# Swapping the head halves of the rotary step by DMA instead of by a permutation matmul

## What is computed

```python
def apply_rope(x, cos, sin):              # x: (..., 64) per head and map
    x1, x2 = x[..., :32], x[..., 32:]
    return concatenate([x1 * c - x2 * s, x1 * s + x2 * c], axis=-1)

qa = apply_rope(qa.reshape(S, 8, 64), cos, sin)
ka = apply_rope(ka.reshape(S, 8, 64), cos, sin)
s = einsum('bqhmd,bkhmd->bhmqk', qa, ka) * scale     # scores of differential attention
```

## Time and profile before

| what | value |
|---|---|
| median of 3 runs | 1937.48 us (1933.66 to 1937.8) |
| the profiled execution's own time | 1934.02 us |
| its span | 1932.2 us |
| TensorE busy | 1889.2 us (98%) |
| VectorE busy | 1299.9 us (67%) |
| ScalarE busy | 921.7 us (48%) |
| GpSimd busy | 233.2 us (12%) |
| mean granted TensorE clock | 0.993 |
| DMA | 177.20 MB, mean 92 GB/s |

### The profile page before, as it was taken

One profiled execution on the slowest core, in us unless ns is written; L12 is line 12 of the kernel. 1 busy time (PEld: TensorE's weight loads), 2 busy tenths in 40 slices (PEclk: granted clock), 3 DMA queues, 4 the chain that ended last, 5 costly groups with the idle time before them and its releaser, 6 DMA issues.

```text
span 1932.2 us, 31506 instructions
## 1 busy us (share of the span) xinstructions
PE 1889.2 (98%) x11358; PEld 1647.4 (85%) x11358; DVE 1299.9 (67%) x1910; ACT 921.7 (48%) x1589; POOL 233.2 (12%) x207
## 2 busy tenths in 40 slices
PE   7999999999999999999999999999999999999998
PEld 6899988778878889998888999888776788999886
DVE  6789832667555678983267989435796677999423
ACT  4355522427556445552243555333387543555323
POOL 2100000220224210000021000002156221000001
PEclk8999999999999999999999999999999999999999
DMA  4132332312211213233222232322321022333321
GB/s 156 66 116 102 112 128 87 102 68 71 94 44 45 87 67 120 98 115 124 87 88 88 88 114 103 131 87 88 115 72 45 21 70 85 110 109 109 119 99 44
DMA packets 36574, 177.20 MB, mean 92 GB/s; under 512 B 12544, under 2 KB 14080, under 8 KB 16016
## 3 DMA queue, kind: packets, MB, share of 16 engines
q1 hardware_dynamic: 35040, 173.76, 26.3%
q10 hardware_dynamic: 1264, 1.80, 0.3%
q0 software_dynamic: 192, 0.59, 0.1%
HBM read 174.04 MB, written 2.10 MB: 91 GB/s over the span
## 4 chain that ended last, share of the span: by engine, by line
PE 92%; DVE 3%; ACT 2%; POOL 1%; issue 1%; DMA 1%; SPq 0%; ACTq 0%; POOLq 0%; DVEq 0%
PE ps L352 29%; PE ps L354 28%; PE ps L353 28%; PE ps L1622 1%; DVE wl L286 1%; ACT wh L282 1%; PE ps L1645 1%; PE ps L1152 1%; PE ps L1224 1%; POOL xg L2461 1%; POOL acc L439 1%; DMA raw<-in_units 1%; PE ps L1351 0%; PE ps L1214 0%; PE ps L1134 0%
## 5 line engine op out<-in xcount | busy, mean ns | idle before, releaser
L352 PE MATMUL ps<-xgh,wh 128*128 128x256 f32 (+1 forms) x1504 | 513.8, 342 | 12.7 <-DVE wl L286 5.1
L354 PE MATMUL ps<-xgh,wl 128*128 128x256 f32 (+1 forms) x1504 | 506.8, 337 | 0.0
L353 PE MATMUL ps<-xgl,wh 128*128 128x256 f32 (+1 forms) x1504 | 506.2, 337 | 0.0
L286 DVE TENSOR_TENSOR wl<-raw,wh 128x2048 fp32r<-128x2048 f32 (+1 forms) x92 | 212.7, 2312 | 359.1 <-ACT wh L282 359.1
L352 PE MATMUL ps<-tmh,wh 128*128 128x256 f32 (+1 forms) x1344 | 411.5, 306 | 0.0
L353 PE MATMUL ps<-tml,wh 128*128 128x256 f32 (+1 forms) x1344 | 410.6, 305 | 0.0
L354 PE MATMUL ps<-tmh,wl 128*128 128x256 f32 (+1 forms) x1344 | 410.1, 305 | 0.0
L282 ACT ACTIVATE wh<-raw 128x2048 fp32r<-128x2048 f32 (+1 forms) x92 | 174.5, 1898 | 364.7 <-PE ps L354 363.2
L352 PEld LDWEIGHTS ps<-xgh,wh 128*128 128x128 f32 x1504 | 286.2, 190 | 48.0 <-DVE wl L286 6.1
L353 PEld LDWEIGHTS ps<-xgl,wh 128*128 128x128 f32 x1504 | 286.1, 190 | 30.1 <-issue 2.2
L354 PEld LDWEIGHTS ps<-xgh,wl 128*128 128x128 f32 x1504 | 286.2, 190 | 29.8
(11 more groups left out here) (310 smaller groups left out, 2584.3 us busy)
## 6 DMA issues: line engine op xcount, KB each, us to landing
raw<-in_units SPq DMA_DIRECT2D x160, 1024.0 KB, 4.9
out<-xg SPq DMA_DIRECT2D x4, 512.0 KB, 4.0
relb<-in_rpb SPq DMA_DIRECT2D x64, 24.0 KB, 2.1
x<-in_xT ACTq DMA_DIRECT2D x2, 512.0 KB, 5.9
raw<-in_units SPq DMA_DIRECT2D x4, 256.0 KB, 6.5
x<-in_xT SPq DMA_DIRECT2D x2, 512.0 KB, 8.0
cosA<-in_rope_a ACTq DMA_DIRECT2D x1, 256.0 KB, 2.6
sinA<-in_rope_a ACTq DMA_DIRECT2D x1, 256.0 KB, 2.9
```

Of the source, the lines that this page charges most:

```text
L286: nc.vector.tensor_tensor(wl[:, c % 2, 0:n], raw[:, c % 2, 0:n], wh[:, c % 2, 0:n].bitcast(F32), ALU.subtract).then_inc(w_lo, 1)
L352: nc.tensor.matmul(dst, lh, rh, start=first, stop=False, skip_group_check=onto)
L353: nc.tensor.matmul(dst, lh, rl, start=False, stop=False, skip_group_check=onto)
L354: return nc.tensor.matmul(dst, ll, rh, start=False, stop=last, skip_group_check=onto)
```

## The change

The permutation products on TensorE are left out. Instead, ScalarE issues four DMAs for each block, each from 32 partitions of `q32` to the 32 partitions that hold the other half of the head, into a new buffer `rq` with two slots. The minus sign moves into the sine table, on the host. VectorE's multiplication by the sine table reads `rq` from SBUF where it read PSUM. The load of `permA` is left out, so the semaphore of the tables counts to 48.

```diff
-        permA = sb("permA", [P, P], F32, diff_mem)
+        rq = sb("rq", [P, 2, SEQ], F32, diff_mem)
...
-        rot_done = sem("rot_done")
+        rot_in = [sem("rot_in0"), sem("rot_in1")]
...
-        def rot_pe(pe, i):
-            pe.wait_ge(q32_done, i + 1)
+        def rot_act(act, i):
+            act.wait_ge(q32_done, i + 1)
             if i >= 2:
-                pe.wait_ge(qs_done, i - 1)
-            nc.tensor.matmul(ps[:, 2 + i % 2, :], permA[:, :], q32[:, i % 2, :],
-                             start=True, stop=True).then_inc(rot_done, 1)
+                act.wait_ge(qs_done, i - 1)
+            for r in range(0, P, 32):
+                o = r ^ 32
+                act.dma_start(rq[r:r + 32, i % 2, :], q32[o:o + 32, i % 2, :]).then_inc(rot_in[i % 2], 16)
...
-            for dst, src in ((cosA, rope_a[0:P, :]), (sinA, rope_a[P:2 * P, :]), (permA, perm_d[:, 0:P])):
+            for dst, src in ((cosA, rope_a[0:P, :]), (sinA, rope_a[P:2 * P, :])):
...
-                rot_pe(pe, i - 2)
-            rot_pe(pe, 6)
...
-                    if v == 0 and t == 0:
-                        rot_pe(pe, 7)
...
                 if i == 1:
                     act.wait_ge(lam_done, 2)
                     nc.scalar.activation(col(C_LAM, 2), col(C_LAM, 2), ACT.Exp).then_inc(lam_exp, 1)
+                rot_act(act, i)
                 if i >= 1:
                     qa_hi_act(act, i - 1)
...
-            dve.wait_ge(rot_done, i + 1)
+            dve.wait_ge(rot_in[i % 2], 64 * (i // 2 + 1))
...
-            nc.vector.tensor_tensor(qs[:, i % 2, :], ps[:, 2 + i % 2, :], sinA[:, :], ALU.mult).then_inc(qs_done, 1)
+            nc.vector.tensor_tensor(qs[:, i % 2, :], rq[:, i % 2, :], sinA[:, :], ALU.mult).then_inc(qs_done, 1)
...
+    turn_sign = np.ones((2 * P, 1), np.float32)
+    turn_sign[P:][np.arange(P) % 64 < 32] = -1.0
...
-        "ident": np.eye(P, dtype=np.float32), "perm": perm, "rope_a": rope_rows(64, P, 0),
+        "ident": np.eye(P, dtype=np.float32), "perm": perm, "rope_a": rope_rows(64, P, 0) * turn_sign,
```

More of the change, by code:

```diff
@@ L1797, in even_pe @@
             norm_pe(pe, 1, 4)
-            pe.wait_ge(even_in, 64)
+            pe.wait_ge(even_in, 48)
             for i in range(2, 8):
@@ L1847, in even_act @@
                     norm_act(act, 1, 4)
-                    act.wait_ge(even_in, 64)
+                    act.wait_ge(even_in, 48)
                 if i == 1:
@@ L1921, in even_dve @@
         def even_dve(dve):
-            dve.wait_ge(even_in, 64)
+            dve.wait_ge(even_in, 48)
             nc.vector.tensor_tensor(lamp, lamb.rearrange("p (a b e) -> p a b e", a=2, b=2)[:, :, 0, :],
@@ L2051, in even_pool @@
         def even_pool(pool):
-            pool.wait_ge(even_in, 64)
+            pool.wait_ge(even_in, 48)
             for i in range(8):
```

## The result

| | kernel before | changed kernel |
|---|---|---|
| median of 9 runs each | 1937.44 us | 1940.96 us |
| lowest and highest | 1932.92 to 1938.04 | 1939.12 to 1941.72 |
| ratio, with 95% interval | | 1.0026 (1.0017 to 1.0035) |
| profiled execution: time, span | 1934.02, 1932.2 | 1940.2, 1938.4 |

The change makes the kernel slower by 0.26% of its time, which is some 5 us, by the ratio, and by 3.5 us by the medians. My forecast was 1938.5 us with a range of 1933.5 to 1943.0.

The account below looks back on a forecast made before the run. The prediction took TensorE as the bound, with VectorE arriving together at the first scores. VectorE's chain 1.1 us later plus 1.7 for a clock fall made +2.8 us on 1935.7: 1938.5 us, range 1933.5 to 1943.0.

Parts of the forecast that it names:

- the late transfers: Rival: even blocks' transfers land in 4.9 us for 2.8, behind the weight load; +2.4, giving 1940.9 us; chance 0.17.
- the signs that I had written under "wrong": Trace signs against the forecast: landings after 5 us, issues above 0.6 us, splits 11 us apart, or first scores before 434.
- What bounds the kernel: First mixer: TensorE and VectorE arrive together at the scores; VectorE's loop slightly longer, 11.19 us a pair against 11.0.
- Part 1, the products: Eight permutation products removed, 6.8 us of TensorE, a gain only as VectorE's chain shortens; the dropped table load counts nothing.
- Part 2, the first rotation: Before block 4: issues and landing make the first sine product 2.1 us later; TensorE idles some 3.3 us.
- Part 3, an iteration: VectorE's loop: reading SBUF beside GpSimd adds 0.55 us an iteration, a pair 12.35 us for 11.19; issues hidden to 0.6.
- Part 3, the landing in even blocks: Even blocks' transfers land 4.85 us behind q32's start, wanted at 5.08: hidden by a hair.
- Part 4, the sum: Splits 12.35 us apart end the last low part at 436.75 for 435.67, 1.1 us later; nothing left of the 6.8.
- the two smaller gaps, at 409 and 421: TensorE's waits for VectorE before block 6 and the first `va` block, about 1.3 us each.
- Part 5, the clock: Behind TensorE's new 3.2 us gap before the scores the clock falls once, at the lower price, 1.7 us.
- Which time that is: Base time for the whole kernel: 1935.7 us, the mean of two groups near 1934 and 1937.6, giving 1938.5 us.

Follow-up runs that it names:

- e4: Changed kernel without transfers, their issues or the wait for them, the sine product reading q32; swap left out: 1935.64 us, ratio 0.9998 to the kernel before.
- e5: Changed kernel with the sine product reading a stale PSUM bank instead of rq, transfers and waits kept: 1941.83 us, ratio 1.0028 to the kernel before.
- e3: Changed kernel with transfers still issued, but the sine product reads q32 without waiting for their landing: 1938.08 us, ratio 1.0000 to the kernel before.
- e9: Changed kernel with one 256 KB DMA of 128 partitions in place of four, halves not swapped: 1937.18 us, ratio 1.0004 to the kernel before.
- e1: Changed kernel with VectorE scaling q32 of even blocks ahead of the next unit's weight split: 1936.46 us, ratio 0.9988 to the kernel before.

## Why the prediction was right, and where its terms were off

The forecast was +2.8 us for the likeliest case, and the measured change is 3.5 by the medians, 5 by the ratio. The direction and the reason held: VectorE's chain sets the first scores, and TensorE's 6.8 us turn into waiting. But I held a change within 0.2% the likeliest (0.61) and gave 0.30 to a slower kernel, which it just became. By the medians the change is 0.18%, inside my likeliest class; by the ratio it is 0.26%, with an interval from 0.17. The 2 us that the sum lacks are those of the rival I named, the late transfers, at 0.17. That 2.8 and 3.5 lie so near each other is in part luck: the profiled executions differ by 4.5 us in this stretch, and the base that I chose was 1.7 us below the median of the result. Two of the signs that I had written under "wrong" also came: transfers landing after up to 5.1 us, and issues above 0.6 us (0.61 in the median) with the high part waiting for ScalarE's queue.

By its own steps, with lengths of the changed kernel's trace:

- *What bounds the kernel.* Right for the end of the stretch, where both engines arrive together, and wrong as a rule for the loop. "VectorE's loop is slightly the longer of the two already" was read from the last pair (11.19 us); the two pairs ahead of it took 13.85 and 13.00, with waits of 2.85 and 2.22 us for the products. The sum did not suffer, since it added pairs of the changed kernel to absolute times. e4 shows what was to be had with VectorE's order and an SBUF operand: with no transfer at all the chain is 1.9 us shorter, not 6.8.
- *Part 1, the products.* Right; that the load left out gives nothing was not tried by itself.
- *Part 2, the first rotation.* I had the first sine product 2.1 us later, by 0.48 us an issue and 2.8 of landing. It came 4.73 us after the first q32 where it was 2.70 before, 2.03 later, out of two errors that cancel: issues of 0.51 to 0.62 and a landing of 2.0. TensorE's wait before block 4 was 3.25 for 3.3.
- *Part 3, an iteration.* 4.47 us was predicted and 4.48 measured, but the reason was only half right. The sine product itself never grew in this kernel (0.681 to 0.693), since GpSimd's product was never running when it started; the sum did, in the iterations of blocks 2, 4 and 6, to 1.58 to 1.60 us, 0.39 more than before and not 0.55. What then sets the high part is the fourth issue on ScalarE, which ends 3.15 us behind q32's start. I had said the issues are hidden up to 0.6 us each; at 0.61 they no longer are. e5 and e4 show both.
- *Part 3, the landing in even blocks: the step that failed.* I had put it at 4.85 us behind q32's start, "hidden by a hair" against 5.08. It was 6.8, for the transfer's 2.8 us was a price without a load in flight. Splits came 13.0 us apart for 12.35, 2.0 us in three pairs; e3 gives 2.2 for the whole. The rival had the place and, at 0.8 a pair for the 0.65 measured, nearly the price, but I took it for unlikely with the argument that the load is nearly half done by then. e9 shows why that is no argument: the transfer comes in about when the load does, whatever the load has behind it when the transfer is issued.
- *Part 4, the sum.* +1.1 was the chain; it was +2.97 (52.77 - 49.80). TensorE's gap before the scores was 4.05 for 3.2. Of the two smaller gaps, at 409 and 421, the first did not show and the second was 1.34: the clock had fallen behind the gap before block 4 too (0.50 from 396 to 400 us) and TensorE arrived later, which cost nothing, as I had said.
- *Part 5, the clock.* It fell, for 1.5 to 2.1 us where 1.7 was counted. Chain and clock together are 5.0 us in the first profile; 4.5 of it arrive at the attention, since the first q32 was 0.29 us earlier than before and the scores followed the last low part 0.21 us sooner. The sum would have been 4.8 with the landing right.
- *Which time that is.* Putting the forecast on the mean of four executions took 1.7 us off it. Later medians of the kernel before, 1936.04, 1935.4 and 1935.62, say that this was the better base for it. The kernel before itself was 1937.44 in the runs of the result, and with the forecast on that median it would have been 1940.2.

The Trainium skill's rule (SBUF — State Buffer, section "Who interferes with whom") that two-input VectorE work and GpSimd's reads exclude each other is borne out by the rows: GpSimd's product beside it grew from 1.27 to 1.67 us, and the sum ended 0.55 us after it (423.21 + 1.67 = 424.88, and 423.83 + 1.60 = 425.43). e1's split shows both orders: 3.00 us where GpSimd had started first, 2.28 where the split had, and then GpSimd's product took 3.27. In the changed kernel this did not decide the time, by e5.

Still open: why one issue in e1 took 1.36 us, and why a transfer behind a load lands only after it. Neither was tried further.

## What to carry to other kernels

Before an operation of the busiest engine is replaced by transfers, follow the chain that shares its deadline: here it ran over VectorE and arrived at the same moment, so without any transfer the gain was 1.9 us and not 6.8. Read every pass of a loop before you say which engine is the longer: here the last one differed from the two ahead of it. A small transfer has two prices, one alone and one beside a large load; issue it ahead of what releases the load (one instruction moved took 4.2 us off the chain), and count the issues on the engine that has other work behind them. Where a new wait of the matmul engine appears, look at the granted clock behind it too.

## What was unexpected of the hardware

- Four transfers of 64 KB from 32 partitions to 32 took 0.51 to 0.62 us of ScalarE's queue each, one of 256 KB over 128 partitions 0.47: the smaller cost more to issue. Alone they landed after 2.0 and 2.3 us.
- Issued behind the start of a 1 MB load on another engine's queue, both kinds landed 6.3 to 7.1 us after the split that releases the load (e9 6.35 to 6.41; the changed kernel 6.7 to 6.8, and 6.7 to 7.1 again), though e9's was issued 1.8 us sooner, and in the changed kernel the load took 5.8 us instead of 4.9.
- A wait of 3.64 us on TensorE was followed by full speed in one execution (a pair of matmuls in 1.10 us) and the same wait of 3.65 us by half speed in another (2.04 us). In e4 a wait of 1.15 us, before block 4, was followed by a granted clock of 0.50 (396 to 398 us). In these runs the length of a wait alone did not tell whether the clock falls behind it.
- VectorE's split of a weight unit took 3.00 us instead of 2.29 when it ran into GpSimd's product of 1.3 us; when the split had started first, GpSimd's product took 3.27 us and the split 2.28 (e1).
